# Two feed-forward products issued k by k, a norm broadcast copied to SBUF, and a later rounding in the Hyena projection

## What is computed

```python
def rmsnorm(x, g):
    y = xf * lax.rsqrt(jnp.mean(xf * xf, axis=-1, keepdims=True) + EPS)
    return (y * g)

def conv_glu(h, lp, rows):
    up = h @ lp['ffn_up']                       # 1024 -> 2 x 2816
    a, gte = up[..., :FFN_HIDDEN], up[..., FFN_HIDDEN:]
    a = dwconv_grid(a, lp['ffn_conv_w'], rows) + lp['ffn_conv_b']
    return (gelu(a) * gte) @ lp['ffn_down']

def mixer_hyena(h, lp):
    u = dwconv1d(h @ lp['w_in'], lp['hy_short_w']) + lp['hy_short_b']
    ...                                         # filters from a small MLP, long convolutions
    return z @ lp['w_out']

x = x + g1 * mixer(rmsnorm(x, lp['norm1']) * (1 + sc1) + sh1)
x = x + g2 * conv_glu(rmsnorm(x, lp['norm2']) * (1 + sc2) + sh2, lp, rows)
```

## Time and profile before

| | us |
|---|---|
| median of 3 runs | 4609.59 |
| lowest, highest | 4608.66, 4614.04 |
| the profiled execution | 4613.63 |
| its span | 4611.8 |

### The profile page before, as it was taken

One profiled execution on the slowest core, in us unless ns is written; L12 is line 12 of the kernel. 1 busy time (PEld: TensorE's weight loads), 2 busy tenths in 40 slices (PEclk: granted clock), 3 DMA queues, 4 the chain that ended last, 5 costly groups with the idle time before them and its releaser, 6 DMA issues.

```text
span 4611.8 us, 52491 instructions
## 1 busy us (share of the span) xinstructions
PE 4115.4 (89%) x22572; PEld 3465.3 (75%) x22572; DVE 2403.8 (52%) x2654; ACT 1024.9 (22%) x1448; POOL 1155.7 (25%) x579
## 2 busy tenths in 40 slices
PE   5899787887989999999969999987676899999998
PEld 3688677777768888888757777776565688888886
DVE  4372355555234444443547556679983354444453
ACT  3152221212132111111133333311111311111112
POOL 1111233233242222222231000013221422222224
PEclk7999799999889999999979999998888899999999
DMA  6511000000212221212122222241221011111111
GB/s 236 164 36 37 21 1 1 1 19 1 83 37 60 61 66 58 60 60 60 51 87 68 89 89 76 77 154 72 112 103 37 23 37 37 37 38 38 38 38 69
DMA packets 309551, 280.55 MB, mean 61 GB/s; under 512 B 9909, under 2 KB 285830, under 8 KB 305831
## 3 DMA queue, kind: packets, MB, share of 16 engines
q1 hardware_dynamic: 309320, 277.19, 18.3%
HBM read 219.48 MB, written 57.67 MB: 60 GB/s over the span
## 4 chain that ended last, share of the span: by engine, by line
PE 72%; DVE 17%; issue 3%; DMA 3%; ACT 2%; POOL 2%; SPq 1%; POOLq 0%; DVEq 0%; ACTq 0%
PE PS L670 53%; DVE piece L1769 8%; PE PS L1837 5%; DVE piece L1194 3%; PE PS L1165 2%; PE PS L1166 2%; PE PS L1161 2%; PE PS L2010 1%; DMA piece<-in_l_ada_w 1%; PE PS L856 1%; DVE piece L1705 1%; PE PS L1610 1%; DVE piece L2178 1%; DVE piece L2206 0%; ACT piece L510 0%
## 5 line engine op out<-in xcount | busy, mean ns | idle before, releaser
L670 PE MATMUL PS<-piece,piece 128*128 128x512 f32 (+1 forms) x13824 | 2790.4, 362 | 78.0 <-POOL piece L545 35.2
L670 PEld LDWEIGHTS PS<-piece,piece 128*128 128x128 f32 x13824 | 2309.1, 191 | 531.8 <-issue 103.8
L653 POOL TENSOR_TENSOR piece<-piece,piece 128x1024 fp32r<-128x1024 f32 (+1 forms) x204 | 506.0, 2481 | 2544.7 <-ACT piece L647 2544.7
L1837 PE MATMUL PS<-piece,piece 128*128 128x256 f32 x1920 | 441.1, 392 | 126.3 <-DVE piece L2464 111.3
L1705 DVE SCALAR_TENSOR_TENSOR piece<-piece,piece,piece 128x1024 f32<-128x1024 f32 x352 | 534.8, 1519 | 12.6
L1837 PEld LDWEIGHTS PS<-piece,piece 128*128 128x128 f32 x1920 | 376.4, 197 | 186.1 <-DVE piece L2464 114.1
L1725 DVE SCALAR_TENSOR_TENSOR piece<-PS,piece,piece 128x1024 f32<-128x1024 f32 x224 | 187.7, 880 | 416.0 <-PE PS L670 416.0
L647 ACT ACTIVATE piece<-piece 128x1024 fp32r<-128x1024 f32 (+1 forms) x204 | 205.4, 1007 | 660.4 <-PE PS L670 613.7
L1194 DVE TENSOR_TENSOR piece<-piece,PS 128x512 f32<-128x512 f32 x288 | 185.3, 684 | 249.6 <-PE PS L1166 192.3
L1702 DVE TENSOR_SCALAR piece<-piece,piece 128x1024 f32<-128x1024 f32 x44 | 35.8, 813 | 514.8 <-ACT piece L1652 514.8
L1655 ACT ACTIVATE piece<-piece 128x1280 f32<-128x1280 f32 x44 | 56.1, 1275 | 607.5 <-DVE piece L1713 607.5
(11 more groups left out here) (237 smaller groups left out, 3581.8 us busy)
## 6 DMA issues: line engine op xcount, KB each, us to landing
piece<-in_l_ffn_up SPq DMA_DIRECT2D x88, 512.0 KB, 3.6
piece<-in_l_w_in SPq DMA_DIRECT2D x44, 512.0 KB, 3.7
piece<-in_l_ada_w SPq DMA_DIRECT2D x44, 512.0 KB, 5.2
piece<-in_l_ada_w SPq DMA_DIRECT2D x18, 1024.0 KB, 7.9
piece<-in_l_ffn_down SPq DMA_DIRECT2D x48, 384.0 KB, 3.0
piece<-filters_s SPq DMA_DIRECT2D x8, 2176.0 KB, 9.8
filters_s<-piece SPq DMA_DIRECT2D x64, 256.0 KB, 2.0
hyena_tokens<-piece SPq DMA_DIRECT2D x24, 640.0 KB, 4.0
```

Of the source, the lines that this page charges most:

```text
L653: eng.tensor_tensor(LO[i % 2][0][:, 0:n], RAW[i % raws][:, 0:n], HI[i % 2][1][:, 0:n], ALU.subtract)\
L670: m = eng.matmul(PS[:, bank + b, 0:n], w, x[:, a:a + n], start=first and n_ == 0, stop=last and n_ == 2)
L1837: m = eng.matmul(PS[:, bank, o * HC:(o + 1) * HC], M[i][o], rhs[i], start=i == 0, stop=i == 1)
```

## The change

There are three edits.

1. `norm` (all three uses): DVE copies `RS` from PSUM to an SBUF tile `RSB` before k = 4 (a step called `back`), and reads `RSB` instead of `RS` for k = 4 to 7. `RSB` is the third of the tiles that held the squares.
2. `conv_glu` (both layers): PE issues items 0 and 1 together, for each k first the product of item 0 and then that of item 1. The product of item 1 waits for `back`. The two modulation products of items 0 and 1 follow k = 1 and k = 4.
3. `mixer_hyena`: `hi(1)` and `lo(1)` are taken out of `early`; ACT does `hi(1)` after the norm has ended, at the start of its Hyena program, and POOL does `lo(1)` after the norm.

```diff
-            DIAG, SS, RS = r.take(NT, P), SQ[1][:, 0:NT], psum(3, N)
+            DIAG, SS, RS, RSB = r.take(NT, P), SQ[1][:, 0:NT], psum(3, N), SQ[2]
...
+            def wait_lo(eng, k, second=False):
+                if second:
+                    eng.wait_ge(ve.sem, ve.at("back"))
...
+                        if k == 4:
+                            eng.tensor_copy(RSB, RS).then_inc(*ve.did("back"))
+                            eng.wait_ge(ve.sem, ve.at("back"))
...
-                            eng.scalar_tensor_tensor(T[k % 4][:, a:a + n], XT[:, k, a:a + n], SCALE_A[:, which, k, j:j + 1], RS[:, a:a + n],
+                            eng.scalar_tensor_tensor(T[k % 4][:, a:a + n], XT[:, k, a:a + n], SCALE_A[:, which, k, j:j + 1], (RSB if k >= 4 else RS)[:, a:a + n],
...
+                ring.ready(eng, 0)
+                for k in range(KD):
+                    for i in range(2):
+                        h_ready(eng, k, i == 1)
+                        if i == 1 and k == 0:
+                            ring.ready(eng, 1)
+                        w = ring.get(i, shape(items[i]))
+                        m = product(eng, 3 * i, (w[0][:, k, :], w[1][:, k, :]), (HH[:, k], HL[:, k]), k == 0, k == KD - 1)
+                        if k == KD - 1:
+                            m.then_inc(*pe.did("used", i))
+                    if NQ and k in (1, 4):
+                        rows((k - 1) // 3)
+                    if NQ and k == KD - 2:
+                        turn(eng, 0)
...
-            early.update(ac=lambda eng: [ring.hi(eng, i) for i in range(2)], po=lambda eng: [ring.lo(eng, i) for i in range(2)])
+            early.update(ac=lambda eng: ring.hi(eng, 0), po=lambda eng: ring.lo(eng, 0))
...
+                ring.hi(eng, 1)
                 for n in range(n_t + 1):
...
-                for n in range(2, n_t):
+                for n in range(1, n_t):
                     ring.lo(eng, n)
```

More of the change, by code:

```diff
@@ L466, in norm @@
             poS = steps("po_norm_sum", [f"add{k}" for k in range(1, KD)])
-            ve = steps("ve_norm_r", ["inv", "diag"])
+            ve = steps("ve_norm_r", ["inv", "diag", "back"])
             names = []
@@ L474, in norm @@
             po = steps("po_norm", [f"lo{k}" for k in po_tiles])
-            def wait_lo(eng, k):
+            def wait_lo(eng, k, second=False):
+                if second:
+                    eng.wait_ge(ve.sem, ve.at("back"))
                 eng.wait_ge(*((ve2.sem, ve2.at(f"lo_p{k}")) if k in LO_ON_VE else (po.sem, po.at(f"lo{k}"))))
@@ L1585, in _, with rows @@
             def _(eng):
+                def rows(q):
+                    eng.wait_ge(s_aw[2], 16 * (q + 2))
+                    for kk in range(KD):
+                        lane = kk % LANES
+                        m = eng.matmul(PS[32 * lane:32 * lane + 32, 6 + q % 2, 0:P], CW[:, kk, :], QW[:, kk, :], start=kk < LANES, stop=kk >= KD - LANES)
+                    m.then_inc(*peQ.did("rows", q))
+                ring.ready(eng, 0)
[12 more added lines that the diff above has]
+                        turn(eng, 0)
                 for i, (kind, j, mp) in enumerate(items):
+                    if i < 2:
+                        continue
                     ring.ready(eng, i)
                     w = ring.get(i, shape(items[i]))
-                    if kind == "a" and j:
+                    if kind == "a":
                         eng.wait_ge(ac.sem, ac.at("line", j - 1))
-                    if kind == "g" and j:
+                    if kind == "g":
                         eng.wait_ge(ve.sem, ve.at("hid", j - 1))
@@ L1599, in _ @@
                         for k in range(KD):
-                            if i == 0:
-                                h_ready(eng, k)
                             m = product(eng, 0 if kind == "a" else 3, (w[0][:, k, :], w[1][:, k, :]), (HH[:, k], HL[:, k]), k == 0, k == KD - 1)
@@ L1606, in _ @@
                             if k == 1 and NQ:
[L1607 to L1612, removed]
+                                rows(q)
+                            if k == KD - 2 and NQ:
                                 turn(eng, q - 1)
```

## The result

The changed kernel takes 4621.86 us in the median of 13 runs (4617.68 to 4634.57), the kernel before 4611.40 in 13 runs beside it (4605.68 to 4615.70). The ratio is 1.0028, with a 95% interval of 1.0021 to 1.0035: slower, by 13 us by the ratio and by 10.5 us between the two medians, and clear of no change. The forecast was 4621.8, that is +12.2 us.

What follows compares the result with a forecast made beforehand. TensorE, busy 89% of the span, was taken as the bound. Layer 1 +5.5, layer 0 +7.1 and Hyena -0.4 sum to +12.2 us: 4609.59 becomes 4621.8, with an 8-in-10 range of 4612 to 4626.

Steps and rivals of the forecast that it cites:

- Feed-forward of layer 1: Layer 1 feed-forward under edit 2: item 2 starts 3.5 us later, plus 2.0 for the clock; +5.5, between +3.0 and +6.5.
- The stop ahead of item 2: Both feed-forwards: PE idles about 4.0 us before item 2, since 1.745 of the 5.74 us weight path is covered.
- The two clock terms: Feed-forwards: low-clock loss after `back`, 2.0 us (1.5 to 2.55), and after the idle before item 2, 2.0 (0 to 2.45).
- the slack that was forecast: Layer 1: item 3's weights ready at 3694.7, item 2 ending at 3695.5, just in time with 0.8 us of slack.
- Feed-forward of layer 0: Layer 0 feed-forward under edit 2: +4.9 for item 2's start and 2.0 for the clock; +7.1 in all, +6.6 to +8.1.
- The wait for `QW`: Layer 0: `QW` for item 2, queued behind `lo(2)`, lands at 1392.8, k = 1 done at 1392.6; replaces a smaller clock loss.
- The copy and the contention: Hyena norm under edit 1: ends 5.9 us later, copy included; from +0.8 to +1.6 (copy alone) up to +6.4.
- The sign "up to 2.7 us": Expected in the changed profile: L532 reading from SBUF takes up to 2.7 us in place of 1.27.
- The prediction's sentence on the Trainium skill: Hyena norm: were four pairs to run in half their 6.42 us, Hyena gains 3.2 more, sum 9.0; rows show no gain.
- Edit 3: Hyena norm: chain starts 6.26 us earlier; less 5.9 this gains 0.4, between 5.5 and -0.1; displaced rounding costs nothing.
- the case that contention costs little or the clock holds: Rival for feed-forwards and Hyena: only the stalls, Hyena keeps 3 to 5 us; +4 to +9, 4613.6 to 4618.6; chance 0.24.
- The gap that might have grown: Rival in the feed-forwards: item 3 late too, clock falls again; another +2 to +5, 4624 to 4627; chance 0.10.

Runs made afterwards that it cites:

- the filler: Changed kernel plus 18 unread extra matmuls of 512 columns between items 1 and 2 in layer 1; 4621.24 us, ratio 1.0020 to the kernel before.
- the unread copy: Kernel before plus the copy of RS to RSB in all three norms, DVE still reading RS for all k; 4617.10 us, ratio 1.0013.

## Why the prediction was right, step by step

**The total.** +12.2 us forecast; the ratio says +13 (9.7 to 16.1), the medians +10.5, and the stretches A, B and D of the two pairs of profiles +12.6 and +12.0. Right. That 4621.86 lies within 0.1 us of the forecast 4621.8 is luck: the forecast started from a median of 4609.59 for the kernel before, which is 4611.40 with 13 runs, and single executions of the changed kernel lie up to 17 us apart.

**Feed-forward of layer 1.** +5.5 forecast, +4.8 and +6.0 measured. The stop ahead of item 2 was forecast at 4.0 us and is 4.10 and 4.12, and item 0's end to item 2's weights took 5.67 where 5.74 was put in. Moving item 0's end forward took the stop away, so the lost cover is the cause. The two clock terms were each put at 2.0 and are not constants. Behind the wait for `back` the first profile lost only 26.39 - 15 x 1.745 = 0.2 us; the second took 28.71 for the same 15 products and lost 2.5. Behind the stop ahead of item 2 2.8 were lost in the first and some 1.9 in the second. Item 3 had the slack that was forecast: with the filler it became the next limit by 0.90 us.

**Feed-forward of layer 0.** +7.1 forecast, +8.6 and +6.7 measured. The sizes that were off are the clock terms again: 8.13 us for three products behind `back` (2.8 lost, 2.0 assumed), 6.04 us for two products of item 2 (2.5 lost). In the second profile it was 6.78 us (1.4 lost) and 5.31 us (1.7 lost). The wait for `QW` is there, hidden by the low clock in item 2, as said. In the second profile, where less was lost to the clock, `QW` was late by 0.25 and, for item 3, by 0.71 us. That it takes the clock's place was right in kind; that this holds the lower end at +6.6 was right by a hair (+6.65 measured).

**The copy and the contention.** Copy 1.489 us forecast from L1717, 1.478 measured. The norm was to end 5.9 us later by the copy and by what the prediction calls the port, DVE and POOL in each other's way; edits 1 and 2 without edit 3 gave +5.8, edit 1 alone +5.6. The model behind it was that a DVE instruction with two tensors in SBUF waits for POOL's instruction in progress. The changed kernel shows it at its plainest (3893 ns for a piece that takes 1272 to 1276 ns where POOL is idle), and the unread copy separates the operand's place from the extra instruction. The sum was right, but the prediction reached it as if all four tiles and POOL's work ran one after the other. In the changed kernel only two of the four larger pieces of the Hyena norm waited (2.46 and 3.89 us); the other two took 1.27. The sign "up to 2.7 us" for such a piece was too low. The prediction's sentence on the Trainium skill ("VectorE: DVE Perf Modes", Rules for kernel authors) asked what the advice to copy first, if many operations follow, would bring here. With four tiles behind the copy it brought nothing: three pairs read from SBUF took 6.04 us against 4.83. The half price in that sentence was the prediction's own supposition; the rule names no factor for an operation on two tensors.

**Edit 3.** 6.26 forecast, 6.20 measured alone; with the 5.9 of the copy and the contention the net was to be -0.4 and is -0.8 and -0.6 in the two pairs. The displaced rounding costs nothing, as said.

**The bounds.** I let the range reach down to 4612 for the case that contention costs little or the clock holds. The contention was there in every profile. The clock did hold behind `back` in layer 1 in one of two profiles, but never behind the stop ahead of item 2. The gap that might have grown, by a late item 3, didn't in layer 1; in layer 0 item 3's own weights weren't late, only its `QW` was, by 0.71 us in the second profile.

**Left open.** Why the profiled execution of the changed kernel took 12.7 us more than the median. The table places some 9 us of it in C (against the kernel before, and 12 against its own second profile), which holds the same matmuls in both kernels. In its windows, where the filter's short products alternate with those of the projection, the granted clock was

```profile
2580.00:2600.00 20.00, 20.00 (x94) 0.91 0.03 8
```

in the kernel before and

```profile
2586.00:2606.00 20.00, 20.00 (x50) 0.50 0.00 1
```

in the changed kernel, at the same place of the program. From ACT's 8th to its 9th copy in C, around these windows, it took 39.6 us at a mean of 0.74 there, and 31.7 us at 0.95 in the kernel before and in the changed kernel's second profile. Edit 3 alone, whose C is 634.6 and 645.0, had 31.7 us at 0.95 and 39.6 at 0.74 there. So it isn't the change that decides it. What does, these runs don't show.

## What to carry to other kernels

When two consumers of a late input are interleaved, look at what starts at the *end* of the first one: here 5.7 us of copy and rounding for the third tile, covered by the second tile's 14 us until the interleaving left 1.7 of them. Order the products so that the pause at the front is filled and the first consumer still ends some products before the second. And before an operand is copied from PSUM to SBUF to free a bank, look at who else works on SBUF at that time: the copy itself was 1.5 us, the reads from SBUF behind it made the norm another 3.6 us longer, without being faster in themselves.

## What the runs showed of the hardware

- A VectorE instruction of 1024 columns with two tensor operands in SBUF that starts while a GpSimd two-operand subtraction runs ends 1.07 to 1.09 us after GpSimd's end, in every such case of the three norms in both kernels. It took 2.40 to 3.99 us accordingly, and 1.27 to 1.29 where no subtraction was under way. With one operand in PSUM it took 1.27 to 1.28 us, beside a running subtraction too (15 of 24 such pieces in the norms of the kernel before).
- A stop of TensorE of 4.0 to 4.1 us was followed by 3.5 to 5.3 us at the lower clock level (four cases, two profiles of the changed kernel), and 1.7 to 2.8 us of work were lost; 4.25 us of filler matmuls in its place kept the clock at 1.00. A stop of 2.1 us behind 3.5 us at the lower level cost between 0.2 and 2.8 us in the same four places. A stop of 2.47 to 2.55 us ahead of k = 4 in layer 1 cost 1.8 us in the kernel before and 3.2 in one profile of edit 3 alone. Such a term needs a range, not a value.
- TensorE's clock can stay at its lower level for 20 us of full business (20.00 of 20.00 us busy) in a stretch where short products alternate with full ones, and in the kernel before, at the same place of the program, it was at 0.91. In two profiles of one kernel the stretch of 640 us around it differed by 12 us, more than the change under study; it had to be kept out by comparing stretches.
